# Samples and output of a hybrid decoder layer in one pass, with cache buffers one deep and w_out loaded in eight pieces

## What is computed

```python
pk = cache_k[l][page_table].reshape(Bs, past_len, A_HEADS, 2, A_DQK)
pv = cache_v[l][page_table].reshape(Bs, past_len, A_HEADS, A_DV)
so_a = _diff_attend(saq, k_all, v_all, pos_s, kpos_s, lam)      # samples, cached and new keys
so_h, S_s = _hgrn2(shq, shk, slf, shi, state_hgrn[l])           # samples, with their states

def _merge(x, o_attn, ag, o_hgrn, hg, subln_g, hgrn_norm_g, lam_init, w_out):
    a = (_rms_norm(o_attn, subln_g) * (1.0 - lam_init)).reshape(B, T, D_ATTN) * jax.nn.silu(ag)
    r = _rms_norm(o_hgrn, hgrn_norm_g).reshape(B, T, D_HGRN) * jax.nn.silu(hg)
    return x + jnp.concatenate([a, r], axis=-1) @ w_out
```

## Time and profile before

| | us |
|---|---|
| median of three runs | 1761.52 (1758.78 to 1763.17) |
| profiled execution, its time | 1758.49 |
| its span | 1756.7 |
| TensorE busy (matmuls) | 1577.5 |
| VectorE, ScalarE, GpSimd busy | 982.8, 753.1, 485.7 |
| mean granted TensorE clock | 0.962 of full speed |

### The profile page before, as it was taken

How to read it: one execution, slowest core, us unless ns; L and a number is a source line. 1 busy time by engine, 2 the same in 40 slices (tenths; PEclk the granted TensorE clock), 3 DMA queues, 4 the chain that set the end, 5 groups by cost and what they waited for, 6 DMA issues and landing times. The chain is left out here.

```text
span 1756.7 us, 25192 instructions
## 1 busy us (share of the span) xinstructions
PE 1577.5 (90%) x9156; PEld 1277.6 (73%) x9156; DVE 982.8 (56%) x2316; ACT 753.1 (43%) x1074; POOL 485.7 (28%) x636
## 2 busy tenths in 40 slices
PE   6799999997999999999999689999999568299998
PEld 5688888886887788778887567767777445177776
DVE  4322222254677667766776489888888624523332
ACT  5333333345444544453445266666666422211110
POOL 1433223341544664466446200000000010121211
PEclk9999999998999999999999889999999869699999
DMA  8444433445010101010100331000000286534442
GB/s 298 179 144 144 144 144 144 179 141 170 26 37 31 55 31 37 30 55 31 37 31 31 116 121 66 30 25 13 14 24 13 82 279 222 162 117 138 150 142 72
DMA packets 79762, 171.48 MB, mean 98 GB/s; under 512 B 9122, under 2 KB 15906, under 8 KB 79650
## 3 DMA queue, kind: packets, MB, share of 16 engines
q1 hardware_dynamic: 79650, 170.00, 28.0%
HBM read 113.35 MB, written 56.62 MB: 97 GB/s over the span
## 5 line engine op out<-in xcount | busy, mean ns | idle before, releaser
L92 PE MATMUL h_banks<-h_w_hi,h_x_hi 128*128 128x512 f32 x1088 | 435.4, 400 | 23.0 <-DVE h_x_lo L651 16.5
L94 PE MATMUL h_banks<-h_w_hi,h_x_lo 128*128 128x512 f32 x1088 | 426.9, 392 | 0.0
L93 PE MATMUL h_banks<-h_w_lo,h_x_hi 128*128 128x512 f32 x1088 | 426.7, 392 | 0.0
L92 PEld LDWEIGHTS h_banks<-h_w_hi,h_x_hi 128*128 128x128 f32 x1088 | 206.6, 190 | 65.9 <-DVE h_x_lo L651 17.3
L94 PEld LDWEIGHTS h_banks<-h_w_hi,h_x_lo 128*128 128x128 f32 x1088 | 206.0, 189 | 44.3
L93 PEld LDWEIGHTS h_banks<-h_w_lo,h_x_hi 128*128 128x128 f32 x1088 | 206.5, 190 | 40.7
L145 POOL TENSOR_TENSOR h_stage_or_levels<-h_stage_or_levels,h_qk_or_hgrn 128x128 f32<-128x128 f32 x192 | 105.8, 551 | 283.2 <-ACT h_stage_or_levels L589 283.2
L1078 ACT ACTIVATE p_scores<-p_scores,p_nmx 128x256 f32<-128x256 f32 (+15 forms) x128 | 153.1, 1196 | 5.6 <-DVE p_nmx L1129 5.4
L1214 PE MATMUL p_ops<-p_V,p_WT 128*128 128x128 f32 x1088 | 146.4, 280 | 8.8 <-ACT p_WT L1087 8.4
L1214 PEld LDWEIGHTS p_ops<-p_V,p_WT 128*128 128x128 f32 x1088 | 132.6, 193 | 15.6 <-ACT p_WT L1087 14.2
L1124 DVE CUSTOM_DVE_ANT_0 p_scores<-p_sps,p_zero 128x512 f32<-128x512 f32 x192 | 122.2, 686 | 15.8 <-PE p_sps L1188 15.6
(11 more groups left out here) (218 smaller groups left out, 2642.4 us busy)
## 6 DMA issues: line engine op xcount, KB each, us to landing
h_stage_or_levels<-in_w_in SPq DMA_DIRECT2D x32, 512.0 KB, 6.3
h_xs_sq_or_tok<-in_xT SPq DMA_DIRECT2D x17, 512.0 KB, 5.9
h_qk_or_hgrn<-in_x SPq DMA_DIRECT2D x17, 512.0 KB, 6.1
tmp_xh_s<-h_x_hi SPq DMA_DIRECT2D x17, 512.0 KB, 3.2
tmp_xl_s<-h_x_lo SPq DMA_DIRECT2D x17, 512.0 KB, 4.4
h_x_hi<-tmp_xh_s SPq DMA_DIRECT2D x17, 512.0 KB, 3.6
h_x_lo<-tmp_xl_s SPq DMA_DIRECT2D x17, 512.0 KB, 4.5
s_kc<-in_cache_k SPq DMA_DIRECT2D x32, 256.0 KB, 3.7
```

Of the source, the lines that this page charges most:

```text
L92: eng.matmul(out, x_hi[:, k, :], w_hi[:, k, :], start=(k == 0), stop=False)
L93: eng.matmul(out, x_hi[:, k, :], w_lo[:, k, :], start=False, stop=False)
L94: mm = eng.matmul(out, x_lo[:, k, :], w_hi[:, k, :], start=False, stop=(k == KD - 1))
```

## The change

`pass_samples` and `pass_output` become one pass, `pass_samples_output`. Its order is a count n of quarters: a quarter is six products (two of the eight k blocks, three products each), eight quarters are a tile, 17 tiles are 136 quarters. Steps of the samples stand behind certain quarters: sample j begins at n = 10 + 11j, its steps are numbered r = 0 to 10, and head h = j - 2 of the recurrence goes with it. All engines follow this count; the program is written out in full, without the loops of the output pass.

```diff
+PERIOD, START, FIRST = 11, 10, 2
+QUARTERS = 8 * NT
+def sample_step(n):
+    j, r = divmod(n - START, PERIOD)
+    return (j, r, j - FIRST) if 0 <= j < DEC_B else (-1, -1, -9)
...
-        kc = sb("kc", [P, AHEAD, NPG, GW])
-        vc = sb("vc", [P, AHEAD, NPG, GW])
+        kc = sb("kc", [P, NPG, GW])
+        vc = sb("vc", [P, NPG, GW])
...
-        sc = sb("sc", [P, 2, NK])
-        PT = sb("PT", [P, 2, NPG + 1, P])
+        sc = sb("sc", [P, NK])
+        PT = sb("PT", [P, NPG + 1, P])
...
+        w_stage = S[:, :, :, :].rearrange("p b h v -> p (b h v)").rearrange("p (n k c) -> p n k c", n=4, k=2)
+        yps = [ps(f"yps{g}", [P, GW]) for g in range(2)]
+        ytp = ps("ytp", [P, 4, P])
+        ktp = ps("ktp", [P, 4, P])
...
         def w_piece(n):
-            return slice(n % 2 * 4, n % 2 * 4 + 4), slice(n // 2 * GW, n // 2 * GW + GW)
+            return slice(n % 4 * 2, n % 4 * 2 + 2), slice(n // 4 * GW, n // 4 * GW + GW)
```

TensorE:

```diff
+            def quarter(i, q):
+                g, b = divmod(q, 4)
+                if q == 0:
+                    pe.wait_ge(s["mT_lo"], 2 * i + 2)
+                if b == 0 and i >= 1:
+                    pe.wait_ge(s["y"], 2 * i - 1 + g)
+                if i == 0:
+                    pe.wait_ge(s["w_lo"], q + 1)
...
+            columns(0, 1)
+            columns(0, 0)
+            for n in range(QUARTERS):
+                i, q = divmod(n, 8)
+                j, r, h = sample_step(n)
+                quarter(i, q)
+                if q == 1 and i < NP:
+                    columns(i + 1, 1)
+                if q == 3 and i < NP:
+                    columns(i + 1, 0)
+                if 0 <= r < NPG:
+                    key_columns(j, r)
+                if r == 4:
+                    scores(j)
+                if r == 7:
+                    weight_columns(j)
+                if r == 9:
+                    values(j)
+                if n == START - 2:
+                    new_columns()
+                if h == -1 and r == 10:
+                    decayed_keys()
+                if 0 <= h < H:
+                    if r == 1:
+                        level_products(h)
+                    if r == 5:
+                        state_rows(h)
+                    if r == 8:
+                        gains(h, 0)
+                    if r == 10:
+                        gains(h, 1)
```

SP. In the opening: pages, tile 0 (`load_y(0)`: o_in, ga, mr), four pieces of `w_out`, tile 1, x of tile 0, four more pieces, the new keys, `keys(0)`, x of tile 1, `load_y(2)`, `vals(0)`, the recurrence's nine inputs, and the state `S`, whose place the pieces of `w_out` had. Then:

```diff
+            sp.wait_ge(s["w_lo"], 8)
+            load(S[:, :, :, :]..., "state_load")
+            for n in range(QUARTERS - 8):
+                i, q = divmod(n, 8)
+                j, r, h = sample_step(n)
+                if q == 1 and i >= 1:
+                    store_y(i - 1)
+                if q == 4:
+                    if i >= 1:
+                        load_x(i + 1)
+                    if i + 3 < NP:
+                        load_y(i + 3)
+                if r == 0 and 1 <= h <= H:
+                    store_state(h - 1)
+                if r == 4 and j + 1 < DEC_B:
+                    keys(j + 1)
+                if r == 10:
+                    store_part(j)
+                    if j + 1 < DEC_B:
+                        vals(j + 1)
```

More of the change, by code:

```diff
@@ L1304, in pass_samples @@
+        yps = [ps(f"yps{g}", [P, GW]) for g in range(2)]
+        ytp = ps("ytp", [P, 4, P])
+        ktp = ps("ktp", [P, 4, P])
+        rowps = ps("rowps", [P, PAST])
+        pps = rowps[:, :].rearrange("p (g t) -> p g t", g=NPG)
+        small = ps("small", [P, 2 * P + DEC_T])
+        ops, pnew, nps = small[:, 0:P], small[:, P:2 * P], small[:, 2 * P:]
         rps = ps("rps", [P, H, DV])
         ups = ps("ups", [P, 4, DV])
[L1307 to L1313, removed]
@@ new lines, in store_state @@
+            def store_state(h):
+                sp.wait_ge(s["state"], 2 * h + 2)
+                sp.dma_start(io["s_s"][:, h].rearrange("b d v -> d b v"), S[:, :, h]).then_inc(s["state_store"], 16)
+            load(pages[:, :], io["page_table"], "pages")
+            load_y(0)
+            load(ng[:, 0], io["subln_g"].partition_broadcast(P).rearrange("p a b -> p (a b)"), "ng")
+            for n in range(4):
+                load_w(n)
+            load_y(1)
+            load_x(0)
+            for n in range(4, 8):
+                load_w(n)
@@ L1418, in _, with own_values @@
+            def own_values(h):
+                if h == 0:
+                    pool.wait_ge(s["load"], 80)
+                    pool.wait_ge(s["new_ps"], 2)
+                else:
                     pool.wait_ge(s["gain_ps"], 2 * h)
@@ L1427, in _, with squares @@
         @block.scalar
         def _(act):
-            def keys_out(j):
-                for g in range(NPG):
-                    act.wait_ge(s["kT_ps"], 4 * j + g + 1)
-                    if g == 0 and j >= 1:
-                        act.wait_ge(s["scores"], 2 * j - 1)
-                    act.activation(KT[:, :, g * PAGE:(g + 1) * PAGE], tps[g % 2][:, :, :], ACT.Copy).then_inc(s["kT"], 1)
+            def squares(i):
+                act.wait_ge(s["o_load"][i % 2], 16 * (i // 2 + 1))
+                after(act, s["o_ss"], i)
+                act.activation(sq[:, :], o_in[:, i % 2], ACT.Square).then_inc(s["o_sq"], 1)
+                act.wait_ge(s["o_ss"], i + 1)
+                after(act, s["o_rs"], i)
+                act.activation(oss[:, 1], oss[:, 0], ACT.Sqrt, bias=eps[:, 0:1], scale=1.0 / DV).then_inc(s["o_root"], 1)
@@ new lines, in _ @@
+            hi_part(0, 0)
+            w_rounded(2)
+            w_rounded(3)
+            squares(1)
+            for n in range(QUARTERS - 8):
+                i, q = divmod(n, 8)
+                j, r, h = sample_step(n)
+                if n < 4:
+                    w_rounded(4 + n)
+                if q == 1:
+                    hi_part(i + 1, 1)
+                if q == 3:
+                    hi_part(i + 1, 0)
+                if q == 5 and i + 2 <= NP:
+                    squares(i + 2)
+                if n == 16:
+                    decays()
+                if 0 <= r < NPG:
+                    keys_out(j, r)
+                if r == 4:
+                    exp_row(j)
+                if h == -1 and r == 10:
+                    key_rows()
+                if h == H and r == 5:
+                    state_stats()
```

786 lines of the change are left out of this document (366 added, 420 removed).

## The result

| | before | changed |
|---|---|---|
| median of the runs, us | 1762.35 (1758.78 to 1764.67) | 1703.08 (1698.6 to 1706.88) |
| span of the profiled execution | 1756.7 | 1700.8 |
| fused pass: first issue of SP to the end | 362.4 | 302.7 |

The ratio is 0.9671 (95% interval 0.965 to 0.9692): 3.3% faster, 0.9 us beside the forecast of 1704 and inside its range. The span shrank by 55.9 us, the part that the change touches by 59.7: its first issue lies at 1398.13 us, 3.9 later than before.

A forecast was written before the change was run, and what follows sets the result against it. TensorE was taken to bound the fused pass: 294.8 us of work plus 10.6 of opening waits gave 305.4 against 362.4, 57.0 less, so 1701.5 profiled and a forecast median of 1704 us (range 1688 to 1730).

The forecast's parts named there:

- TensorE as the bound, products at 0.234 us: Fused pass: TensorE bounds it; 48 products take 11.24 us, 17 such tiles 191.2 us.
- The samples' work and the insertions: TensorE's sample and state work between quarters, 61.1 us; 68 switches to and fro at 0.08, 5.4 us (0 to 17.7).
- Opening: From the fused pass's first issue to the first product: 14.0 us, bounds 13 and 17.
- The wait at sample 0: TensorE waits 7.0 us for sample 0's scores, since tile 3's o_in stands behind the state's load.
- The decays: At n = 16 the differences and one Exp of 3072 columns sit ahead of hi_part on ScalarE: 1.4 us.
- The clock after a stop: After the wait at sample 0's scores, the next products run at half clock again: 2.2 us.
- Eight waits for banks gone: Output products: the eight waits of 0.8 us for VectorE's additions vanish; the bill has none.
- Covers: After the opening, other work hides keys (8.3 us issue plus landing, one deep), values, eleven table loads: no cost.
- (b): Rival: no wait at sample 0, the state's load lets small transfers by; 1694 us, down to 1688; chance 0.20.
- (c): Rival: in-order queues collide, 1.5 to 3 us a step, or insertions cost their upper bound; 1716 to 1730; chance 0.20.
- (d): Rival: one-deep keys late at every sample, TensorE stands 5 us each, x8 = 40; 1744 us; chance 0.09.
- (e): Rival: as (d), and each stop also halves the clock for about 10 us; 1784 us, slower; chance 0.04.

The follow-up runs named there:

- e1: Changed kernel with tile 3's loads (o_in, ga, mr) issued ahead of the state's load: 1696.91 us.
- e2: Changed kernel with the state's load issued at step 15, behind the keys of sample 1: 1697.08 us.
- e11: Changed kernel with e2's later state load, gains loaded first, second w_out split later, decays at step 19, level products at step 22: 1691.78 us.
- e10: Changed kernel with the next sample's keys issued behind its values' loads at r = 10, so really late: 1785.18 us, ratio 1.0137.
- e3: Kernel before, with only the wait ahead of the output's products set to the addition that frees the bank: 1753.23 us, ratio 0.995.
- e6: Changed kernel with two key buffers, keys of sample j + 2 issued at r = 4 of sample j: 1705.23 us.
- e5: Changed kernel with the next sample's keys issued at r = 7 in place of r = 4: 1703.76 us.
- e12: e11 with VectorE's first two splits of w_out behind both low parts of tile 0: 1692.16 us.

## Why the prediction was right

- **TensorE as the bound, products at 0.234 us.** Right. 116 of the 136 quarters lie in the 228.4 us without a wait; their 696 products take 163.0 us at that pace.
- **The samples' work and the insertions.** Mechanism right, price too high. The remaining 65.4 us of the 228.4 were forecast as 72.1: 26 groups of columns 12.5, seven samples 35.0, four heads 19.6, small transposes 0.4, 58 insertions 4.6. The steady stretch (timeline of TensorE, changed kernel) shows the smaller prices:

```profile
1508.48 0.60 PE L1859 MATMUL f_rowps<-ident,f_sc 128*128 128x128 f32 x4
...
1508.94 0.48 PE L1819 MATMUL f_yps<-f_w_hi,f_mT_hi 128*128 128x512 f32 x1
1509.26 0.39 PE L1820 MATMUL f_yps<-f_w_lo,f_mT_hi 128*128 128x512 f32 x1
...
1510.88 0.80 PE L1819 MATMUL f_yps<-f_w_hi,f_mT_hi 128*128 128x512 f32 x1
1511.51 0.39 PE L1820 MATMUL f_yps<-f_w_lo,f_mT_hi 128*128 128x512 f32 x1
...
1523.14 0.60 PE L1837 MATMUL f_ktp<-ident,f_kc 128*128 128x128 f32 x4
1523.49 0.47 PE L1819 MATMUL f_yps<-f_w_hi,f_mT_hi 128*128 128x512 f32 x1
```

Start to start, a group of four key transposes costs 0.35 us (1523.14 to 1523.49) and was priced 0.5; 28 of them make some 3.7 of the 6.7 us (0.37 each on average). A group of the output's columns is the same four transposes and was priced 0.48. The weights and their small transpose cost 0.46 (1508.48 to 1508.94) for 0.6. Two matmuls of a gain cost 0.46 and stretch the next product from 0.234 to 0.63 (1510.88 to 1511.51). Behind any other group that product takes 0.32 (1508.94 to 1509.26), so an insertion is worth 0.08, as chosen; the groups had been priced with tails that products hide.
- **Opening.** Mis-sized: 16.7 us for 14.0, just inside the stated 17. Two terms were too small. VectorE waits 6.62 us for ng ahead of its sum, a load that stands behind tile 0's in the new order, and GpSimd's first multiplication starts 9.00 us behind the first issue, for 7.76 in the kernel before. And the splits do not lie beside the gating, as the bill had it: TensorE's second transposes start at 1412.34 us, released by VectorE's low part, which stands behind two splits of 3.91 us, while the gating had ended at 1410.60. The next two splits, with GpSimd idle, took 2.36. Timeline of the changed kernel:

```profile
1404.89 0.23 DVE L1740 TENSOR_SCALAR f_ng<-f_ng 128x128 f32<-128x128 f32 x1 [6.62 <-DMA f_ng<-in_subln_g]
1405.04 0.68 DVE L1615 TENSOR_REDUCE f_oss<-f_sq 128x4 f32<-128x512 f32 x1
...
1407.78 3.91 DVE L1635 TENSOR_TENSOR f_w_lo<-f_S,f_w_hi 128x1024 fp32r<-128x1024 f32 x2 [0.80 <-ACT f_w_hi L1550]
...
1408.48 2.12 POOL L1486 TENSOR_TENSOR f_o_in<-f_o_in,f_ga 128x512 f32<-128x512 f32 x1
...
1415.07 2.36 DVE L1635 TENSOR_TENSOR f_w_lo<-f_S,f_w_hi 128x1024 fp32r<-128x1024 f32 x2 [0.25 <-ACT f_w_hi L1550]
```

- **The wait at sample 0.** Right in place, cause and releaser: 7.3 us for the 7.0 of the forecast, by the order of state and tile 3 (e1 and e2). That the size fits so well is in part luck, since both ends came over 3 us late. Counted from the first issue, SP issued the state at 38.4 us for 33 to 35, it landed at 49.8 for 44.5 and the o_in of tile 3 at 50.5 for 46.5; TensorE was ready at 45.4 for 42.2, and the scores began at 52.7 for 49.2. **The decays**: 2.0 for 1.4 us, with the cause as said (e11).
- **The clock after a stop.** Priced 2.2 us; e10 gives the same as the mean of seven stops. At sample 0 itself it was about 1.6 (estimated from the starts of scores and products against those of later samples). Behind the decays the bill had the stop and no clock: by the same estimate it cost 1.9 us more there.
- **Eight waits for banks gone.** Right (e3 shows their worth, 6 to 12 us).
- **Covers.** Right: no key load is waited for, and a second buffer changes nothing. The issue takes 3.7 us for four (priced 4.6) and the landing 3.3 (3.7). The pass has 17 table loads and not eleven, 20.5 us more than before and not 12.8; they too lie beside products, and from 1467 us on TensorE waits for none of them.
- **Closing** 5.3 for 4.5.

Set against each other, opening +2.7, the twenty quarters up to 1467.1 us +1.6 (52.2 for 50.6), the long stretch -6.7, closing +0.8, and 1.0 that the sum had twice (the two groups of columns ahead of the first product stand in the opening too) make -2.6, to rounding the 302.7 for 305.4. The sum came so close by errors that cancel. Of the signs one just failed: behind the first 14 us TensorE was busy 0.94 of the time and not over 0.95, by the opening and the two stops. (The bill's 17 x 11.24 is 191.1 and not 191.2, and 1701.5 + 3.0 is 1704.5.)

Of the rivals, (b) said that the wait would not come; it came, but 1697 us is where e1 and e2 stand with most of it gone. (c) did not occur: no step after 1467 us waits. **(d) and (e)** describe e10: with the keys late the one-deep buffer costs 82 us. The advice to double-buffer (Trainium skill, Trainium Kernel Development and Optimization, Best Practices) did not bear here, and e6 with e5 shows the condition: the buffer came free so early that issue and landing fit behind other work. That each late load also costs clock (Trainium skill, TensorE: Matmul & The Clock Gate, HAM oscillation) is what e10's windows show, at 2.2 us a stop. On ScalarE the table loads stayed at 1.28 us each with no drain, 0.2 us of idle time ahead of sixteen of them in all; the drain of 1.38 us that the Trainium skill gives (ScalarE: Activation LUTs, What ACT_TABLE_LOAD costs) shows nowhere here:

```profile
L1541 ACT ACT_TABLE_LOAD x8 | 10.3, 1283 | 0.1
L1561 ACT ACT_TABLE_LOAD x8 | 10.3, 1283 | 0.1
```

## What to carry to other kernels

Where one pass leaves TensorE waiting on short hops between engines and another keeps it full, putting steps of the one between pieces of the other is worth far more than joining them end to end (52 us against 7 here, with the samples' steps strictly in a row); price it by TensorE's own start-to-start times and then walk each in-order queue for what stands ahead of the first steps. A load like the state's (2.1 MB in pieces of 0.5 KB), needed late, must not stand on the queue ahead of a small one that is needed soon, and a long ScalarE instruction not ahead of a short copy that TensorE waits for. Before calling a buffer too shallow, compare when it is free with issue plus landing, and check in the trace when the load was really issued.

## What the hardware showed that I had not expected

**VectorE's split and GpSimd's multiplication hold each other up.** Both read two operands from SBUF. In e11's opening GpSimd's two multiplications and VectorE's split of w_out overlap; in e12 they do not (timelines, e11 then e12):

```profile
1411.39 1.27 POOL L1484 TENSOR_TENSOR f_o_in<-f_o_in,f_ng 128x512 f32<-128x512 f32 x1 [7.37 <-DVE f_ng L1742]
...
1411.63 2.11 DVE L1636 TENSOR_TENSOR f_w_lo<-f_S,f_w_hi 128x1024 fp32r<-128x1024 f32 x1 [0.32 <-ACT f_w_hi L1551]
...
1412.74 2.13 POOL L1487 TENSOR_TENSOR f_o_in<-f_o_in,f_ga 128x512 f32<-128x512 f32 x1
```

```profile
1405.92 1.26 POOL L1484 TENSOR_TENSOR f_o_in<-f_o_in,f_ng 128x512 f32<-128x512 f32 x1 [7.38 <-DVE f_ng L1742]
...
1407.27 1.26 POOL L1487 TENSOR_TENSOR f_o_in<-f_o_in,f_ga 128x512 f32<-128x512 f32 x1
...
1411.04 4.62 DVE L1636 TENSOR_TENSOR f_w_lo<-f_S,f_w_hi 128x1024 fp32r<-128x1024 f32 x4
```

In e11 the second multiplication takes 2.13 us and the split 2.11; in e12 the multiplication takes 1.26 and four splits 4.62, 1.16 each. The records of e11 fit taking turns: 1412.66, the end of the first multiplication, plus 1.1 is the split's end at 1413.74, and that plus 1.13 is the second's at 1414.87. As expected, TensorE's transposes of the gated half start 0.86 us earlier (11.55 us behind the first issue for 12.41), and the theory of a slow first use falls. The first product then waits for the split and stands 0.4 us later, and the time is the same. The page SBUF — State Buffer of the Trainium skill (SBUF: two separate sides) has this rule: a VectorE instruction with two SBUF inputs and a GpSimd instruction that reads SBUF share a port pair as an exclusive lock. The rows agree. In the changed kernel it cost the opening some 1.5 us: what TensorE waited for stood behind two splits of 3.91 us in place of 2.36.

**The issue behind the state's load is held.** After that load (2.1 MB in 0.5 KB pieces, landing 11.4 us after its issue) the next issue on SP took 7.74 us, 8.30 in e1, 6.89 in e2, 6.10 in e11 and 5.30 in e12, whether it was a load or a store; the other issues of the changed kernel's fused pass took 0.3 to 0.6 us for the most part and 1.31 at most. The earlier trace rows had 3.81 for one key load at that place, so in the fused pass the hold is twice as long. Whether it is the small pieces, the size of the one load or what else fills the DMA queues, no run here separates.
